# A fused two-block transformer kernel: units and modulation sums of the first attention in other steps, the index weights' product by held weights, the final row sums behind the key's, and the last expert row set mixed singly

## Chip, cores and metric

One NeuronCore of a Trainium2 chip. The metric is device time in microseconds of one execution.

## What is computed

Input is a sequence of 256 tokens with 1024 channels (and 256 context tokens). Two blocks run one after the other. The first: modulated RMS norms, eight-head attention over the tokens and the context with a relative bias, a gated spatial mix beside it, an output projection, two MLPs with squared ReLU and a convolution module between them. The second, cut to what the change touches:

```python
parts = split(modulate(rms_norm(x, norm_attn), sh1, sc1) @ w_in)   # mq mk mv dq dk dv iq ik iw
ik_n = ik * rsqrt(mean(ik * ik) + EPS)
rel = relu(einsum('bqhd,bsd->bqhs', iq, ik_n))
score = einsum('bqh,bqhs->bqs', iw * IDX_HEADS ** -0.5, rel)       # then top-k keys for dsa
...
s = einsum('bthpd,hpnd->bthpn', h @ w_query, sub_keys)             # top 16 of 128 x 128 experts
act = gelu(einsum('btd,bthkd->bthk', h, u_emb[e_idx]))
y = einsum('bthk,bthkd->btd', g * act, v_emb[e_idx])
out = rms_norm(x + g2 * y, norm_final)
```

`mod = silu(c) @ w_ada + b` gives all shifts, scales and gates of the norms.

## The kernel before, in words

Channels lie on the 128 partitions (x is xT, eight tiles of 128 x 256) until the expert stage, where tokens do. Every weight matrix is cut into **units** of 128 x 1024 numbers, two to a transfer of 1 MB into four slots of `ring` (SP's queue). A product is made in three passes of a shortened type: ScalarE converts the unit's high part (L1083, `WB<-ring`), DVE subtracts it from the weights for the low part (L473, the **split**), and TensorE multiplies high by high, high by low and low by high (`rows`, L1570 to L1572: 24 products of 256 columns; `toks_unit`, L1610 to L1612: 12 of 512). WB holds three units, so conversion and split run up to three units ahead (`ahead`), in program order on each engine, and each waits for the product of three units back.

The 128 **modulation sums** of this part (L458, `mods`) are DVE's: a slice of 128 x 1024 weights times a row, added up. `beside[i]` says how many stand behind the split at unit i. Two slices come in one transfer of 1 MB into slots 4 and 5 of `ring`, asked for when the slice pair before last has been used.

The **first attention** runs in 18 steps of `head_steps`, written once for each engine: in step i TensorE makes the scores of head i (L1726), turns the exponentials of head i-1 (L1733) and multiplies those of head i-2 by the values (L1741). DVE adds the bias and takes the maximum (L631, L634), ScalarE copies the context half (L1175) and takes the exponential (L1183); the turned tile is copied by ScalarE (even heads) or DVE (odd ones, L639). Behind a step stands the unit that `fill` names: the gate's (w_in block 1: g, a gelu on ScalarE behind the last), k (block 3), u (block 0), and the first half of the output projection (w_out 0: o0 to o3). `gate_steps` normalises the gate on DVE in steps 5 to 9 (its root is ScalarE's, in step 9), `between_a` mixes it on TensorE in step 11 (L1800), `aside_a` finishes it on DVE (L706, L709), `cat_hi` and `cat_lo` write it as high and low part. `weigh` divides the attention by its sums once a half of the tokens has its last head. The second half of the output projection (o4 to o7) and `into_x` (L693, the residual) follow.

The **index stage** comes behind the norm b2: w_in2 block 6 in units 0 to 3 (iq, iq, ik, iw), ScalarE's eight squares for the last norm "fin", their sum over channels by GpSimd and TensorE (`mean_of_sum`), the key's own row sum (L1898), roots on ScalarE, reciprocals on DVE (L485). iw is made with the tokens' tiles as held weights and four columns (L1907 to L1909: 48 products). Then w_in2 blocks 0, 1 and 2 with `pick_steps` between them, which makes the index scores and finds the chosen keys by eight rounds of maxima.

In the **expert stage** 256 row sets of 1 MB are gathered (L1516), two to a lot. DVE takes the products with the tokens (L1017), ScalarE gelu, gate and a diagonal matrix for both (L1403, L1407, L1413), TensorE adds diagonal times rows up in PSUM (L1973). `finish` makes the residual, the mean square and the scaling of 128 tokens, and SP writes them out.

Numbers of steps, units and heads are counted from 0.

## Time and profile before

| | |
|---|---|
| runs | 1613.29, 1614.20, 1614.34 us; median 1614.2 |
| profiled execution | 1613.14 us; its span 1611.8 us |
| busy, share of the span | PE 88%, DVE 75%, ACT 45%, POOL 21% |
| gathers (software queue) | 268.45 MB, 40.2% of 16 engines |
| other transfers | 207.37 MB, 34.9% |
| mean granted clock of PE | 0.974 |

A row of the timeline has the start, the time busy, the engine, the line of the kernel, the operation with what it writes and reads, how many instructions it merges, and in brackets the idle time before it with what ended it. "PE" is TensorE, "ACT" ScalarE, "POOL" GpSimd, "SPq" an issue of SyncE's queue. Granted clock 1.0 is 2.4 GHz.

### The profile page before, as it was taken

The page shows a single profiled execution, that of the slowest core. Times are in us where ns is not written, and L with a number is a line of the kernel's source. Part 1 is how long each engine was busy: PE and PEld are TensorE (multiplying, and loading weights), DVE is VectorE, ACT ScalarE, POOL GpSimd, SP SyncE. Part 2 cuts the span into 40 slices and gives each one's busy share as a digit, 9 for nine tenths or more (in the row PEclk, how much of TensorE's full clock was granted, in tenths as well). Part 3 has the DMA queues.
Part 4 walks back from the last instruction along what each step waited for, and adds up shares of the span by engine and source line. Part 5 has one row for each costly group of instructions (what it writes and reads, how often), then busy time and mean ns, then how long its engine had stood idle before and what let it go on. Part 6 is the DMA issues. An engine that isn't in the chain of part 4 may idle for free.

```text
span 1611.8 us, 20802 instructions
## 1 busy us (share of the span) xinstructions
PE 1412.7 (88%) x7592; PEld 1034.8 (64%) x7592; DVE 1212.1 (75%) x2373; ACT 728.5 (45%) x1636; POOL 340.1 (21%) x313
## 2 busy tenths in 40 slices
PE   9899899999998999998999879978777777777776
PEld 3777789999987899997878756633332332222222
DVE  6966788887997788877866697877777787777644
ACT  4455365555567655544334544434333333333322
POOL 1100010001000100002001134464444444444430
PEclk9999899999999999998999989999999999999999
DMA  9752359998520499993522369999999999999994
GB/s 390 315 188 79 145 194 337 342 342 313 190 98 3 155 337 339 343 337 108 202 88 103 118 267 419 419 420 420 419 421 420 420 421 420 420 420 419 421 420 208
DMA packets 66055, 477.15 MB, mean 296 GB/s; under 512 B 7329, under 2 KB 7329, under 8 KB 8737
## 3 DMA queue, kind: packets, MB, share of 16 engines
q0 software_dynamic: 36864, 268.45, 40.2%
q1 hardware_dynamic: 29088, 207.37, 34.9%
q8 instruction: 60, 0.98, 0.2%
q14 instruction: 41, 0.34, 0.1%
q10 hardware_dynamic: 2, 0.01, 0.0%
HBM read 474.75 MB, written 1.05 MB: 295 GB/s over the span
## 4 chain that ended last, share of the span: by engine, by line
PE 47%; DMA 27%; DVE 17%; ACT 5%; issue 3%; POOL 1%; ACTq 0%; POOLq 0%; DVEq 0%
DMA row_h<-in_uv,crow 21%; PE ps L1973 7%; PE ps L1570 6%; PE ps L1572 5%; PE ps L1571 5%; DMA row_x<-in_uv,crow 4%; DVE HID L794 4%; PE ps L1854 4%; PE ps L1853 4%; PE ps L1851 4%; DVE WB L473 4%; PE ps L1556 2%; ACT WB L1083 1%; PE ps L1610 1%; DMA ring<-in_stream 1%
## 5 line engine op out<-in xcount | busy, mean ns | idle before, releaser
L473 DVE TENSOR_TENSOR WB<-ring,WB 128x1024 fp32r<-128x1024 f32 x232 | 287.5, 1240 | 92.5 <-ACT WB L1083 89.5
L1083 ACT ACTIVATE WB<-ring 128x1024 fp32r<-128x1024 f32 x232 | 243.4, 1051 | 127.9 <-PE ps L1854 85.1
L1570 PE MATMUL ps<-hH,WB 128*128 128x256 f32 x920 | 268.4, 292 | 7.4 <-DVE WB L473 5.2
L1973 PE MATMUL ps<-ring,P 128*128 128x512 f32 x448 | 214.1, 623 | 66.1 <-ACT P L1413 64.7
L1571 PE MATMUL ps<-hL,WB 128*128 128x256 f32 x920 | 261.5, 284 | 0.0
L1572 PE MATMUL ps<-hH,WB 128*128 128x256 f32 x920 | 261.5, 284 | 0.0
L1973 PEld LDWEIGHTS ps<-ring,P 128*128 128x128 f32 x448 | 84.3, 197 | 189.6 <-ACT P L1413 99.4
L1403 ACT ACTIVATE On<-On 128x2 f32<-128x2 f32 x128 | 26.0, 203 | 377.4 <-DVE On L1017 377.3
L1017 DVE CUSTOM_DVE_ANT_0 ring<-ring,cT 128x1024 f32<-128x1024 f32 x112 | 136.4, 1226 | 76.6 <-DMA ring<-in_uv,crow 75.6
L1570 PEld LDWEIGHTS ps<-hH,WB 128*128 128x128 f32 x920 | 177.6, 193 | 12.7 <-DVE WB L473 6.7
L1571 PEld LDWEIGHTS ps<-hL,WB 128*128 128x128 f32 x920 | 177.8, 193 | 2.2 <-issue 2.2
L1572 PEld LDWEIGHTS ps<-hH,WB 128*128 128x128 f32 x920 | 177.6, 193 | 0.0
L458 DVE CUSTOM_DVE_ANT_0 ring<-ring,crow,cols 128x1024 f32<-128x1024 f32 x128 | 163.3, 1283 | 9.0 <-DMA ring<-in_um 8.8
L1516 POOL DMA_INDIRECT ring<-in_uv,crow x112 | 123.9, 1106 | 202.9 <-PE ps L1973 164.0
L1470 POOL TENSOR_TENSOR sq<-sq 128x256 f32<-128x256 f32 x30 | 33.3, 1110 | 553.6 <-ACT sq L1088 551.6
L1851 PE MATMUL ps<-XB,WB 128*128 128x256 f32 x512 | 144.9, 283 | 0.0
L1853 PE MATMUL ps<-XB,WB 128*128 128x256 f32 x512 | 144.9, 283 | 0.0
L1854 PE MATMUL ps<-XB,WB 128*128 128x256 f32 x512 | 144.9, 283 | 0.0
L1851 PEld LDWEIGHTS ps<-XB,WB 128*128 128x128 f32 x512 | 98.3, 192 | 0.0
L1853 PEld LDWEIGHTS ps<-XB,WB 128*128 128x128 f32 x512 | 98.3, 192 | 0.0
L1854 PEld LDWEIGHTS ps<-XB,WB 128*128 128x128 f32 x512 | 98.3, 192 | 0.0
L1107 ACT ACTIVATE HID<-ps 128x256 f32<-128x256 f32 (+1 forms) x102 | 39.9, 391 | 124.6 <-PE ps L1572 114.3
(297 smaller groups left out, 2775.4 us busy)
## 6 DMA issues: line engine op xcount, KB each, us to landing
ring<-in_stream SPq DMA_DIRECT2D x116, 1024.0 KB, 6.0
ring<-in_um SPq DMA_DIRECT2D x66, 1024.0 KB, 7.3
ring<-in_wm SPq DMA_DIRECT2D x4, 1024.0 KB, 13.0
bias<-in_bias SPq DMA_DIRECT2D x2, 2048.0 KB, 15.2
HID<-in_um SPq DMA_DIRECT2D x4, 512.0 KB, 18.3
ring<-in_uv,crow POOLq DMA_INDIRECT x112, 27.5
xT<-in_xT SPq DMA_DIRECT2D x1, 1024.0 KB, 9.1
cT<-in_cxT SPq DMA_DIRECT2D x1, 1024.0 KB, 14.4
```

Source lines behind the costliest of these rows:

```text
L458: ve.tensor_tensor_reduce(wk, wk, crow[:, layer // 2, :], 1.0, col[f"bm{layer}"][:, m:m + 1], ALU.mult, ALU.add, M[:, layer, m:m + 1]).the ...
L473: ve.tensor_tensor(unit_dst(j, 1), unit_src(j), f(unit_dst(j, 0)), ALU.subtract).then_inc(s_lo, 1)
L1017: ins = ve.tensor_tensor_reduce(u, u, hN[:, n, :], 1.0, 0.0, ALU.mult, ALU.add, dots[:, h, k0 + i:k0 + i + 1])
L1083: se.activation(unit_dst(j, 0), unit_src(j), ACT.Copy).then_inc(s_hi, 1)
L1516: nc.gpsimd.indirect_dma_start(row_ap[row_of[g]], None, A["uv"], bass.IndirectOffsetOnAxis(ap=eu[:, h, k0 + i:k0 + i + 1], axis=0)).then_i ...
L1570: te.matmul(o, wh[:, c], hi[:, kt, :], start=(kt == 0), stop=False)
L1571: te.matmul(o, wh[:, c], lo[:, kt, :], start=False, stop=False)
L1572: mm = te.matmul(o, wl[:, c], hi[:, kt, :], start=False, stop=(kt == 7))
L1851: te.matmul(o, wh[:, c], rH[d % 2][:, k, :], start=(d == 0 and h == 0 and k == 0), stop=False, skip_group_check=True)
L1853: te.matmul(o, wh[:, c], rL[d % 2][:, k, :], start=False, stop=False, skip_group_check=True)
L1854: mm = te.matmul(o, wl[:, c], rH[d % 2][:, k, :], start=False, stop=(d == 7 and k == 3), skip_group_check=True)
L1973: mm = te.matmul(ps[4 + 2 * n + q][:, :], diag[:, g % 8, :], row_ap[row_of[g]][:, 1024 + q * 512:1536 + q * 512], start=(g % 128 == 0), st ...
```

## The change

- First attention: units u2 and u3 stand in steps 10 and 11, not 9 and 10; o0 to o3 in steps 14 to 17 (before 13, 14, 16, 17); the mix's products in step 12, its two halves on DVE in steps 12 and 13 with a tile each; gelu in step 11. The division by the sums stands a step earlier, the low part where it was; in step 17 both parts stand behind the unit. Of the modulation sums, units g0 to g3 have two each (before one), k2, u0, u1 and k3 one each (before none); o1 and o2 have one (before two each on o0 to o4). Units o4 and o5 are split ahead of the residuals.
- Index stage: iw is a `rows` unit with 24 products of 256 columns; its four rows are copied and turned by two small products behind w_in2's first unit. The conversion of the third unit stands ahead of the squares. The key's row sum, root and reciprocal stand ahead of the final norm's. The eight final scalings of x stand two to a unit behind units 1 to 4 of w_in2 blocks 0 and 1, whose eight units have one modulation sum each (before two on the first four); the pick stands ahead of the sum.
- End: of the last lot each row set has its own gelu, gate and diagonal; `finish_last` works in two halves of 512 channels on DVE and ScalarE, and the last 128 tokens go out in two transfers.

```diff
@@ -357,20 +359,20 @@
         beside = [0] * NU
-        for u, n in enumerate((2, 2, 2, 2, 1, 1, 1, 1, 1, 1)):
+        for u, n in enumerate((2, 2, 2, 2, 1, 1, 2, 2, 2, 2, 1, 1, 1, 1)):
             beside[4 + u] = n
-        for u, n in enumerate((2, 2, 2, 2, 2)):
-            beside[first["w_out", 0] + u] = n
+        for u in (1, 2):
+            beside[first["w_out", 0] + u] = 1
         for l in range(2):
             for k in range(48):
                 beside[first[f"ff1_{l}", 0] + 4 + k * 7 // 6] = 1
-        for u in range(4):
-            beside[first["w_in2", 0] + u] = 2
+        for u in range(8):
+            beside[first["w_in2", 0] + u] = 1
         assert sum(beside) == NM
         emptying = []
...
@@ -415,8 +417,8 @@
         fill = {0: [("w_in", 3, 1)], 1: [("w_in", 1, 0)], 2: [("w_in", 1, 1)], 3: [("w_in", 1, 2)], 4: [("w_in", 1, 3)],
-                5: [("w_in", 3, 2)], 6: [("w_in", 0, 0)], 7: [("w_in", 0, 1)], 8: [("w_in", 3, 3)], 9: [("w_in", 0, 2)],
-                10: [("w_in", 0, 3)], 13: [("w_out", 0, 0)], 14: [("w_out", 0, 1)], 16: [("w_out", 0, 2)], 17: [("w_out", 0, 3)]}
+                5: [("w_in", 3, 2)], 6: [("w_in", 0, 0)], 7: [("w_in", 0, 1)], 8: [("w_in", 3, 3)], 10: [("w_in", 0, 2)],
+                11: [("w_in", 0, 3)], 14: [("w_out", 0, 0)], 15: [("w_out", 0, 1)], 16: [("w_out", 0, 2)], 17: [("w_out", 0, 3)]}
...
@@ -638,12 +636,16 @@
                     if due:
-                        out(due.pop())
+                        n = due.pop()
+                        cat_lo(4, n, ps[4 + n][:, :], ("A", n))
                     if i - 2 in last_head:
-                        due.append(last_head.index(i - 2))
+                        n = last_head.index(i - 2)
+                        weigh("A", n, a_pv["A", last_head[n]], a_p["A", last_head[n]])
+                        due.append(n)
+                    aside(i)
                     if i == 17:
-                        out(due.pop())
-                    aside(i)
+                        n = due.pop()
+                        cat_lo(4, n, ps[4 + n][:, :], ("A", n))
                     yield
...
@@ -695,23 +697,24 @@
             def aside_a(i):
-                if i == 11:
+                if i == 12:
                     for n in range(2):
                         p = row_bank(("gmix", n))
                         V.wait_ge(*g_mix[n])
                         V.wait_ge(s_bsp, 16)
-                        V.wait_ge(s_gelu_u, 1)
                         for g in range(4):
                             c = slice(g * 128, g * 128 + 128)
-                            V.then_inc(ve.scalar_tensor_tensor(out=gsq[:, c], in0=p[:, c], scalar=col["lng"][:, g:g + 1],
+                            V.then_inc(ve.scalar_tensor_tensor(out=gsq[n][:, c], in0=p[:, c], scalar=col["lng"][:, g:g + 1],
                                                                in1=bsp[:, c], op0=ALU.mult, op1=ALU.add))
-                        V.wait_own()
+                if i == 13:
+                    V.wait_own()
+                    V.wait_ge(s_gelu_u, 1)
+                    for n in range(2):
                         g_out.then_inc(ve.tensor_tensor(mixed[n].rearrange("p (g c) -> p g c", g=4),
-                                                        gsq.rearrange("p (g c) -> p g c", g=4),
+                                                        gsq[n].rearrange("p (g c) -> p g c", g=4),
                                                         uT[:, :, n * 128:n * 128 + 128], ALU.mult), n)
+                    for n in range(2):
                         V.wait_ge(*g_out[n])
-                if i == 12:
...
@@ -730,7 +733,10 @@
             for u in range(4):
+                if u < 2:
+                    unit(unit_at["w_out", 1, u])
                 into_x(1, u)
+            for u in (2, 3):
...
@@ -860,26 +866,23 @@
-            for u in range(3):
+            for u in range(4):
                 unit(i0 + u)
                 if u == 1:
                     copy_out(("w_in2", 6, 1, 0), iq[:, 1, :], row_bank(("w_in2", 6, 1, 0))[:, 0:256])
-            r1 = rstd("fin")
             r = rstd("ik")
             V.wait_ge(*out_a["w_in2", 6, 2, 0])
             ve.scalar_tensor_tensor(out=ik, in0=ik, scalar=8.0 ** -0.5, in1=r, op0=ALU.mult, op1=ALU.mult).then_inc(s_ik, 1)
-            unit(i0 + 3)
-            for j in range(2):
-                V.wait_ge(*dense["iw", j])
-                out_v.then_inc(ve.tensor_scalar(iw[:, j, :], ps[4 + j][:, 0:4], 0.5, None, ALU.mult), ("iw", j))
-            for kt in range(8):
+            r1 = rstd("fin")
+
+            def fin(kt):
                 x_done.then_inc(ve.scalar_tensor_tensor(out=xT[:, kt, :], in0=xT[:, kt, :], scalar=col["fg"][:, kt:kt + 1],
                                                         in1=r1, op0=ALU.mult, op1=ALU.mult), ("fin", kt))
 
             def pick_steps():
...
@@ -913,8 +916,17 @@
                         copy_out(name, dst[:, u, :], row_bank(name)[:, 0:256])
-                    unit(first["w_in2", b] + u)
+                    i = first["w_in2", b] + u
+                    ahead(i)
+                    if (b, u) == (0, 0):
+                        V.wait_ge(s_iwt, 1)
+                        ve.tensor_scalar(iw, ps[4][:, 0:8].rearrange("p (j c) -> p j c", j=2), 0.5, None,
+                                         ALU.mult).then_inc(s_iw, 1)
                     next(pick, None)
+                    unit(i)
+                    if 1 <= 4 * b + u <= 4:
+                        for kt in range(2):
+                            fin(2 * (4 * b + u - 1) + kt)
...
@@ -1037,6 +1050,26 @@
+
+            def finish_last():
+                ms, halves = sums[:, 63:64], [slice(q * 512, q * 512 + 512) for q in range(2)]
+                for q, c in enumerate(halves):
+                    V.wait_ge(*((s_mix, 256) if q else (s_m0, 1)))
+                    V.then_inc(ve.tensor_tensor(hN[:, 1, c], ps[6 + q][:, :], g2row[:, c], ALU.mult))
+                    V.wait_own()
+                    ve.tensor_tensor(xN[:, 1, c], xN[:, 1, c], hN[:, 1, c], ALU.add).then_inc(s_x1, 1)
+                V.wait_ge(s_nf, 16)
+                for q, c in enumerate(halves):
+                    V.wait_ge(s_x1, q + 1)
+                    V.then_inc(ve.tensor_tensor(hN[:, 1, c], xN[:, 1, c], nfrow[:, c], ALU.mult))
+                    if q == 0:
+                        V.wait_ge(s_sq1, 1)
+                        ve.tensor_scalar(ends_m[0], ends_m[0], EPS, None, ALU.add).then_inc(s_se, 1)
+                V.wait_ge(s_msr, 2)
+                ve.reciprocal(ms, ms).then_inc(s_rms, 1)
+                V.wait_ge(s_rms, 1)
+                V.wait_own()
+                ve.tensor_scalar(xN[:, 1, halves[0]], hN[:, 1, halves[0]], ms, None, ALU.mult).then_inc(s_y, 1)
...
@@ -1336,10 +1369,11 @@
+            i0 = first["w_in2", 6]
+            ahead(i0)
             for kt in range(8):
                 square("fin", kt)
-            i0 = first["w_in2", 6]
-            for u in range(3):
+            for u in range(4):
                 ahead(i0 + u)
...
@@ -1412,6 +1447,32 @@
+            def gelu_last(l):
+                n, h, k0 = LOTS[l]
+                for i in range(2):
+                    k, g = k0 + i, 2 * l + i
+                    S.wait_ge(s_dot, l + i + 1)
+                    S.then_inc(se.activation(dots[:, h, k:k + 1], dots[:, h, k:k + 1], ACT.Gelu))
+                    S.wait_ge(s_gate, 8 * n + h + 1)
+                    S.wait_own()
+                    S.then_inc(se.activation(wts[:, h, k:k + 1], dots[:, h, k:k + 1], ACT.Copy, scale=gates_[:, h, k:k + 1]))
+                    S.wait_own()
+                    S.wait_ge(s_mix, g - 7)
+                    se.activation(diag[:, g % 8, :], ident[:], ACT.Copy, scale=wts[:, h, k:k + 1]).then_inc(s_dg, 1)
+
...
@@ -1890,24 +1950,17 @@
-            for u in range(2, 3):
+            for u in range(2, 4):
                 rows(i0 + u, ("w_in2", 6, u, 0), normed("b2"), (hH, hL))
+            T.wait_ge(s_isq, 1)
+            moment.then_inc(te.matmul(moment_bank["ik"], onesn[:], sq[:, 0, :], start=True, stop=True), "ik")
             mean_of_sum("fin")
-            T.wait_ge(s_isq, 1)
-            T.wait_ge(*r_root["fin"])
-            moment.then_inc(te.matmul(ps[2][:, 0:256], onesn[:], sq[:, 0, :], start=True, stop=True), "ik")
-            i = i0 + 3
-            T.wait_ge(s_lo, i + 1)
-            T.wait_ge(s_hi, i + 1)
-            for j in range(2):
-                r = slice(j * 128, j * 128 + 128)
-                for kt in range(8):
-                    c = slice(kt * 128, kt * 128 + 4)
-                    o = ps[4 + j][:, 0:4]
-                    te.matmul(o, hH[:, kt, r], WB[:, i % 3, 0, c], start=(kt == 0), stop=False)
-                    te.matmul(o, hH[:, kt, r], WB[:, i % 3, 1, c], start=False, stop=False)
-                    mm = te.matmul(o, hL[:, kt, r], WB[:, i % 3, 0, c], start=False, stop=(kt == 7))
-                dense.then_inc(mm, ("iw", j))
+
+            def turn_iw():
+                T.wait_ge(*out_a["w_in2", 6, 3, 0])
+                for j in range(2):
+                    mm = te.transpose(ps[4][:, 4 * j:4 * j + 4], iw_rows[:, 128 * j:128 * j + 128], ident[0:4, 0:4])
+                mm.then_inc(s_iwt, 1)
...
@@ -2088,10 +2145,13 @@
-            for n in range(2):
-                P.wait_ge(s_y, n + 1)
-                sp.dma_start(out[0, n * 128:n * 128 + 128, :], xN[:, n, :]).then_inc(s_out, 16)
-            P.wait_ge(s_out, 32)
+            P.wait_ge(s_y, 1)
+            sp.dma_start(out[0, 0:128, :], xN[:, 0, :]).then_inc(s_out, 16)
+            P.wait_ge(s_y, 2)
+            sp.dma_start(out[0, 128:256, 0:512], xN[:, 1, 0:512]).then_inc(s_out, 16)
+            P.wait_ge(s_y1, 1)
+            sp.dma_start(out[0, 128:256, 512:1024], xN[:, 1, 512:1024]).then_inc(s_out, 16)
+            P.wait_ge(s_out, 48)
```

DVE in step 2 of the first attention, before (L631 and L634 score and maximum, L458 the modulation sum, which the order calls ISA, with its read-out):

```order
L631 SCALAR_TENSOR_TENSOR P<-ps,bias 128x256
L634 TENSOR_REDUCE sums<-P 128x1
L639 COPY PT<-ps 128x512
L473 TENSOR_TENSOR WB<-ring,WB 128x1024
L458 ISA ring,M<-ring,crow,cols 128x1024
L458 ISA M 128x1
L631 SCALAR_TENSOR_TENSOR P<-ps,bias 128x256
```

and in the change:

```order
L629 SCALAR_TENSOR_TENSOR P<-ps,bias 128x256
L632 TENSOR_REDUCE sums<-P 128x1
L637 COPY PT<-ps 128x512
L475 TENSOR_TENSOR WB<-ring,WB 128x1024
L460 ISA ring,M<-ring,crow,cols 128x1024
L460 ISA M 128x1
L460 ISA ring,M<-ring,crow,cols 128x1024
L460 ISA M 128x1
L629 SCALAR_TENSOR_TENSOR P<-ps,bias 128x256
```

A second modulation sum stands between the split and the score of the next head.

DVE around the first unit of the output projection, before (L603 the low part of the mix, L693 the residual):

```order
L603 TENSOR_TENSOR XB<-sq,XB 128x4x128 x2
L631 SCALAR_TENSOR_TENSOR P<-ps,bias 128x256
L634 TENSOR_REDUCE sums<-P 128x1
L473 TENSOR_TENSOR WB<-ring,WB 128x1024
L458 ISA ring,M<-ring,crow,cols 128x1024
L458 ISA M 128x1
L458 ISA ring,M<-ring,crow,cols 128x1024
L458 ISA M 128x1
L693 SCALAR_TENSOR_TENSOR xT<-ps,M,xT 128x256 x2
L631 SCALAR_TENSOR_TENSOR P<-ps,bias 128x256
```

and in the change (L605 the low part, L629 the score, L475 the split, L695 the residual):

```order
L605 TENSOR_TENSOR XB<-sq,XB 128x4x128 x2
L629 SCALAR_TENSOR_TENSOR P<-ps,bias 128x256
L632 TENSOR_REDUCE sums<-P 128x1
L637 COPY PT<-ps 128x512
L475 TENSOR_TENSOR WB<-ring,WB 128x1024
L695 SCALAR_TENSOR_TENSOR xT<-ps,M,xT 128x256 x2
L629 SCALAR_TENSOR_TENSOR P<-ps,bias 128x256
```

The two sums are gone; the score stands behind the low part as before, and a turned head's copy has come in ahead of the split.

DVE in the index stage, before (L870 the key, L874 iw, L876 the final scaling, L890 the pick's first score):

```order
L485 RECIPROCAL rr<-rr 128x256 x2
L870 SCALAR_TENSOR_TENSOR HID<-HID,rr 128x256
L473 TENSOR_TENSOR WB<-ring,WB 128x1024
L874 TENSOR_SCALAR sums<-ps 128x4 x2
L876 SCALAR_TENSOR_TENSOR xT<-xT,cols,rr 128x256 x8
L473 TENSOR_TENSOR WB<-ring,WB 128x1024
L458 ISA ring,M<-ring,crow,cols 128x1024
L458 ISA M 128x1
L458 ISA ring,M<-ring,crow,cols 128x1024
L458 ISA M 128x1
L890 TENSOR_SCALAR cT<-ps,sums 128x128
```

and in the change (L487 reciprocals, L875 the key, L475 the split, L923 iw, L893 the pick, L460 the modulation sum):

```order
L487 RECIPROCAL rr<-rr 128x256
L875 SCALAR_TENSOR_TENSOR HID<-HID,rr 128x256
L487 RECIPROCAL rr<-rr 128x256
L475 TENSOR_TENSOR WB<-ring,WB 128x1024
L923 TENSOR_SCALAR sums<-ps 128x8
L893 TENSOR_SCALAR cT<-ps,sums 128x128
L460 ISA ring,M<-ring,crow,cols 128x1024
L460 ISA M 128x1
L510 COPY HID<-ps 128x256
L475 TENSOR_TENSOR WB<-ring,WB 128x1024
L893 TENSOR_SCALAR cT<-ps,sums 128x128
```

The key's reciprocal is followed by the key at once; the scalings have left this place (they stand two behind a unit from the next one on), and the pick stands ahead of one sum, not behind two.

## Rows read from the trace of the kernel before

**Rows 1.** The page's chain that ended last: shares of the span by line.
```profile
DMA row_h<-in_uv,crow 21%; PE ps L1973 7%; PE ps L1570 6%; PE ps L1572 5%; PE ps L1571 5%; DMA row_x<-in_uv,crow 4%; DVE HID L794 4%; PE ps L1854 4%; PE ps L1853 4%; PE ps L1851 4%; DVE WB L473 4%; PE ps L1556 2%; ACT WB L1083 1%; PE ps L1610 1%; DMA ring<-in_stream 1%
```

**Rows 2.** Windows: stretch, its length, busy us by engine, PEclk, DMA share, GB/s.
```profile
764.25:793.31 29.06, 27.63 (x201) 25.33 (x201) 27.36 (x60) 10.41 (x13) 1.14 (x1) 1.00 0.52 183
1000.00:1100.00 100.00, 88.92 (x319) 49.19 (x318) 79.83 (x201) 45.76 (x133) 49.47 (x43) 0.97 1.01 420
180.00:190.00 10.00, 8.38 (x49) 8.20 (x49) 6.93 (x13) 1.54 (x2) 0.00 (x0) 0.62 0.13 43
190.00:200.00 10.00, 6.92 (x57) 6.53 (x56) 6.68 (x12) 2.62 (x4) 0.00 (x0) 1.00 0.52 200
```

**Rows 3.** Timeline of DVE, first attention: start us, us, engine, line, what, idle before.
```profile
101.25 1.23 DVE L473 TENSOR_TENSOR WB<-ring,WB 128x1024 fp32r<-128x1024 f32 x1 [1.23 <-ACT WB L1083]
...
102.40 1.28 DVE L458 CUSTOM_DVE_ANT_0 ring<-ring,crow,cols 128x1024 f32<-128x1024 f32 x1
...
103.60 0.42 DVE L631 SCALAR_TENSOR_TENSOR P<-ps,bias 128x256 f32<-128x256 f32 x1
...
106.57 1.23 DVE L473 TENSOR_TENSOR WB<-ring,WB 128x1024 fp32r<-128x1024 f32 x1 [1.83 <-ACT WB L1083]
...
146.70 1.23 DVE L596 TENSOR_TENSOR sq<-sq,sums 128x1024 f32<-128x1024 f32 x1
```

**Rows 4.** Timeline of ACT, step 3 of the first attention.
```profile
104.78 0.72 ACT L1183 ACTIVATE P<-P,sums 128x512 f32<-128x512 f32 x1 [1.44 <-DVE sums L634]
```

**Rows 5.** Timeline of PE, first attention: query products, then waits.
```profile
100.99 1.12 PE L1726 MATMUL ps<-HID 64*128 64x512 f32 x2
...
106.29 1.12 PE L1726 MATMUL ps<-HID 64*128 64x512 f32 x2
...
179.07 1.11 PE L1733 MATMUL ps<-ident,P 128*128 128x128 f32 x4 [3.19 <-ACT P L1183]
...
194.53 0.36 PE L1684 MATMUL ps<-XB,WB 128*128 128x256 f32 x1 [1.50 <-DVE XB L603]
```

**Rows 6.** Timeline of ACT, the gate's root in step 9.
```profile
144.83 1.28 ACT L1238 ACT_TABLE_LOAD   x1
146.13 0.30 ACT L1238 ACTIVATE sums<-sums,eps 128x8 f32<-128x8 f32 x1
```

**Rows 7.** Timeline of DVE, last residual of the output projection.
```profile
209.03 0.88 DVE L693 SCALAR_TENSOR_TENSOR xT<-ps,M,xT 128x256 f32<-128x256 f32 x2 [1.31 <-PE ps L1686]
```

**Rows 8.** Timeline of PE: third index unit, w_in2's first unit, its value unit u2.
```profile
746.11 0.39 PE L1570 MATMUL ps<-hH,WB 128*128 128x256 f32 x1 [2.42 <-DVE WB L473]
...
760.83 0.56 PE L1570 MATMUL ps<-hH,WB 128*128 128x256 f32 x1
...
796.57 0.50 PE L1610 MATMUL ps<-WB,hH 128*128 128x512 f32 x1
```

**Rows 9.** The page's DMA issues: a slice of modulation weights, us to landing.
```profile
ring<-in_um SPq DMA_DIRECT2D x66, 1024.0 KB, 7.3
```

**Rows 10.** Timeline of ACT ahead of the third index unit.
```profile
740.82 2.55 ACT L1088 ACTIVATE cT<-xT 128x256 f32<-128x256 f32 x8
```

**Rows 11.** Timeline of DVE, index stage: reciprocals, final scalings.
```profile
751.74 3.54 DVE L485 RECIPROCAL rr<-rr 128x256 f32<-128x256 f32 x2 [2.33 <-ACT rr L1094]
...
761.08 3.25 DVE L876 SCALAR_TENSOR_TENSOR xT<-xT,cols,rr 128x256 f32<-128x256 f32 x8
```

**Rows 12.** Timeline of all engines at the end.
```profile
1594.85 3.70 PE L1973 MATMUL ps<-ring,P 128*128 128x512 f32 x8 [1.25 <-ACT P L1413]
...
1598.62 0.20 ACT L1403 ACTIVATE On<-On 128x2 f32<-128x2 f32 x1 [3.53 <-DVE On L1017]
...
1599.83 3.70 PE L1973 MATMUL ps<-row_h,P 128*128 128x512 f32 x8 [1.27 <-ACT P L1413]
...
1603.56 1.29 DVE L1027 TENSOR_TENSOR cT<-ps,g2row 128x512 f32<-128x512 f32 x2 [4.97 <-PE ps L1973]
...
1609.16 0.34 SPq L2093 DMA_DIRECT2D out<-xN  x1
```

69 lines of the change are left out of this document (42 added, 27 removed).

## The prediction

> **What bounds the kernel now.** I read the chain of waits first, then a table of windows, then each engine's timeline in the three places that the change touches. The chain says that the expert stage is a matter of transfers: 21% of the span goes to rows gathered into row_h alone [rows 1]. In a window inside that stage the transfer engines are busy all the time at 420 GB/s [rows 2]. An expert row set lands every 2.4 us there (1 MB at 420 GB/s, an estimate from that row), however early it was asked for. So what ends the kernel is the time at which the gathers begin, plus a constant, plus what lies behind the last row. Time saved ahead of the gathers should pass through in full; time saved inside that stage is worth nothing; time saved behind its last row counts in full.
>
> Ahead of it TensorE is busy nearly without a gap, except in the first attention's second half and at the index projection. The rows show both.
>
> **First attention, steps 1 to 8: the modulation work that moves in.** In the change, eight of the 24 modulation sums of this stretch leave the output projection: four go in as second sums of steps 1 to 4, four as single ones of steps 5 to 8. DVE's timeline shows the cost of one step: weight split at 101.25, modulation sum at 102.40 (so the split costs 1.15), score at 103.60 (a sum costs 1.20), next split at 106.57 [rows 3]. On ScalarE the exp starts at 104.78 [rows 4]; the conversion of the next weights stands behind it, and the next split behind that. This is a closed loop: split, sum, score, max, exp (1.18 after the score), conversion and next split (1.79 after the exp): 5.32 us. TensorE's own step, 100.99 to 106.29, is 5.30 [rows 5], so the two just match. With two sums the loop is 6.52.
>
> Steps 1 to 4 therefore run ahead of TensorE's need by less and less: the split of step 4 comes at 102.45 + 2 x 6.52 = 115.5 instead of 111.9. The exp of head 3 ends too late for its transpose by 0.7, that of head 4 by a further 1.2, so TensorE enters step 5 1.9 late. Steps 5 to 8 keep one sum each and have the gate's vector operation of 1.23 as well [rows 3]; their loop is 1.15 + 1.20 + 1.2 + 2.97, about 6.55, with a copy in two of them. Walking it on, the exp of head 9 comes near 147.7, and TensorE, which has no projection unit in step 9 now, stands from about 145.4 to 148.65: a wait of 3.2 us that is new. Its unit u2 starts at 150.0 where it started at 141.3, though now with step 10's work.
>
> **Steps 9 to 17: what comes back.** The gelu's table load (1.28 by the root's [rows 6]) moves a step on with unit u3, and the mix's products too. The first out-projection unit then starts near 169.6. Four units follow in four consecutive steps with hardly a stop, since no double sums stand between score and split on DVE and the normalisation by the softmax sums stands a step earlier. Before, TensorE waits 3.19 for the exp of head 14 and 1.50 for the second half's input [rows 5], and for banks behind it; these go, except for about 1.9 ahead of the second half, where the last difference on DVE now stands behind a split and a residual. The second half is then four units of 2.9 with little between them. I get the last residual at 200.2 where the trace has 209.03 [rows 7]: 8.8 us earlier at the full clock.
>
> The clock takes some of it. Right after the 3.19 wait the stretch 180 to 190 has a granted clock of 0.62 [rows 2], so much of it is at 1.2 GHz; after the 2.42 wait at 746 [rows 8] the next units are slower as well. I take one such stretch of some 8 us after the new 3.2 wait. It makes unit u2 3.5 later, of which the ScalarE chain of table loads hides about half: 2.0. A second, short one around the last wait I take at 0.8. **Term 1: -8.8 + 2.8 = -6.0.** Its bounds: -8.8 (no slow stretch) and 0 (the lengthened loop is not made good). The Trainium skill, TensorE: Matmul & The Clock Gate, section on HAM oscillation, says that groups of products divided by waits start at the lower clock time after time; by that the new waits would each cost, and the term would lie nearer its upper bound. The 3.19 row and the 0.62 behind it agree with it; whether the shorter waits count, these rows leave open.
>
> A table load takes 1.28, and the root behind it starts 1.30 after the load did [rows 6]. The Trainium skill, ScalarE: Activation LUTs, section What ACT_TABLE_LOAD costs, gives 2.66 for a switch with its drain; by that the three loads of steps 9 to 12 would put up to 4 us more on the chain and term 1 would be -2. I go by the row.
>
> The transfers of the second sums have room: the slice for step 3 is asked for at 99.5 and needed at 110.1, and the median slice lands 7.3 after its issue [rows 9].
>
> **Index projection.** Before: the third index unit starts at 746.11 after a wait of 2.42 for DVE's split [rows 8], since eight squares of 2.55 us stand ahead of the weights' conversion on ScalarE [rows 10]. Then two row sums, then 48 small products up to 760.83 [rows 8]. In the change one conversion stands ahead of the squares, so this unit starts at 743.6 and ends at 746.5; the fourth, now 24 products with held weights, starts at 747.4 (its bank is released by a DVE copy behind a split) and ends at 750.3; the key's row sum follows at 750.3, the final one at 751.1, and w_in2's first unit at 751.7, some 9 us earlier. The pick's first product no longer waits for anything but the key (ready at 753.7).
>
> DVE takes over as the bound, and this decides the term. It has both reciprocals from 751.74 [rows 11]; in the change it starts the same two at 751.5 and is done with them and the key at 755.4. Before, from the end of the scalings at 764.25 to the split at 793.31, it is busy for 27.4 of 29.06 us [rows 2]; with the gaps of issue between its instructions this is 28.0 us of work. The change keeps this work and puts the eight final scalings of 3.25 [rows 11] in between: 755.4 + 28.0 + 3.25 + 0.2 = 786.8, so 6.5 earlier. TensorE's unit that needs it started at 796.57 [rows 8]; by the same walk it starts at 789.7, so 6.9 earlier, and from there TensorE is the bound again, as before. One modulation sum a unit in place of two changes nothing in the total, since both kinds of unit lie inside this stretch. The waits of about 2 us that TensorE has in it may lower its clock; I take 0.9 for that. **Term 2: -6.0**, bounds -7.3 and -3 (a slow stretch of some 8 us right where TensorE becomes the bound again).
>
> **The tail.** Before, the last two rows' weights come together: gelu at 1598.62, products of both rows 1599.83 to 1603.5 [rows 12]. TensorE is free from 1598.55 (1594.85 + 3.70). In the change the last row but one can be mixed from 1598.55 to 1600.40 and the last from there to 1602.25: 1.28 earlier. Behind it, before, DVE works from 1603.56 until the output goes out at 1609.16 [rows 12]: 5.6 us. In the change halves pipeline: product and addition for half 0 behind the first half of the last product (1601.4 to 1602.7), for half 1 to 1604.0; its square on ScalarE to 1604.9, root 1605.15, reciprocal (behind the norm product) 1605.7, last scaling 1606.3, on two engines. The second output leaves one issue of 0.34 later, at 1606.7: 2.5 earlier than before, and I add 0.1 for its smaller size. **Term 3: -2.6**, bounds -3.3 and -1.3 (only the earlier mix).
>
> **Sum.** -6.0 - 6.0 - 2.6 = -14.6. The profiled execution took 1613.14 (span 1611.8), so 1598.5 for one like it; the median of the runs shown, 1614.2, lies 1.1 higher: 1599.6.
>
> **The rivals.**
> 1. The longer loop of steps 1 to 8 is not made good: term 1 is 0. For it: the loop and TensorE's step match to 0.02, so each of the eight sums is felt somewhere; against it, the out-projection's waits [rows 5] are there to take it up. 1614.2 - 8.6 = 1605.6.
> 2. No slow stretch follows the new waits, and everything walks as at 2.4 GHz: -8.8 - 6.9 - 2.6 = -18.3, so 1595.9.
> 3. Slower: the clock. If the new 3.2 wait in step 9 holds TensorE at 1.2 GHz through to the end of the second half, the work there (eight heads at 2.35, ten units at 2.87, the mix at 2.0: 49.5 at full clock) takes as long again, less the 8 us of waits it fills: +41 against the walk, so 1614.2 - 18.3 + 41 = 1636.9. It decides against the change once the low-clock time exceeds the forecast's by about 29 us. Against it: at 190 to 200 the clock was back [rows 2] although a wait of 1.5 lies there [rows 5]. A milder version gives a result close to no change.
> 4. The index gain is swallowed: the pick's sums on DVE gate the second attention in another order, and only 0 to 1 us of term 2 arrives: 1605. Against it: both feed the same loop and nothing of DVE's is added there.
>
> **How the numbers follow.** Forecast 0.58, rival 1 0.12, rival 2 0.13, rival 3 0.05 (half of it within 0.2%), rival 4 0.07, and 0.05 for a mix of 1 and 4 near 1611, within or just outside 0.2%. The forecast's own spread from the bounds is about 1596 to 1604. The range 1594.8 to 1606.6 takes in rivals 1 and 2 and leaves out about 0.13. A measurement of this kernel can tell 0.2% (3.2 us) from no change. Faster 0.91, same 0.05, slower 0.04.
>
> **What would show it.** In the changed profile: DVE's splits in steps 2 to 4 some 6.5 apart; TensorE's wait for an exp of about 3 us near 145, and whether the clock drops behind it; the last first-attention residual near 202 to 204; w_in2's first unit near 746 (751.7 less what term 1 gives); 420 GB/s from the first full gather window on; first and last row sets of the mix 1.85 apart; the last output issued some 8 us after the last gelu, where it was 10.5. It is wrong if the gathers begin earlier by 12 us and the end does not, or if the first attention ends later than 209.

## The result and the profile after

| | before | changed |
|---|---|---|
| median of the runs | 1613.74 us (1612.52 to 1614.34, 4 runs) | 1597.92 us (1595.59 to 1599.38, 4 runs) |
| ratio | | 0.9896, 95% interval 0.9883 to 0.9908 |
| profiled execution, span | 1613.14, 1611.8 | 1597.58, 1596.3 |
| granted clock of PE, mean | 0.974 | 0.978 |

The changed kernel takes 15.8 us less by the medians (their quotient is 0.9902, inside the interval) and 15.5 by the two spans. The forecast was 14.6 less, 1599.6, with a range of 1594.8 to 1606.6.

Laid side by side, the traces say where the 15.5 went. The output projection's last residual starts 6.0 earlier, though the first query product starts 1.0 later (84.34 and 85.34); over all traces of this study that start lies anywhere from 84.1 to 85.7, so the 1.0 is chance. The stand-in products ahead of the index stage (products whose result nobody reads, which TensorE makes while a norm is being worked out) start 5.9 earlier, the last pick product 12.1, the first row mix 12.1, the last gelu 12.2, the last output issue 15.2. So the three places have 5.9, 6.2 and, with what lies behind the last issue, 3.3.

Windows of the changed kernel, columns as in [rows 2]: two stretches behind new waits, the two that answer to 180 to 200, and the gathers.

```profile
118.50:123.80 5.30, 5.28 (x25) 5.30 (x26) 3.44 (x7) 4.18 (x7) 0.00 (x0) 0.50 0.92 340
151.00:155.00 4.00, 4.00 (x21) 4.00 (x22) 2.35 (x4) 3.09 (x4) 0.00 (x0) 0.57 0.54 223
180.00:190.00 10.00, 9.73 (x84) 9.49 (x82) 9.92 (x17) 2.85 (x5) 0.00 (x0) 1.00 0.49 170
190.00:200.00 10.00, 8.77 (x73) 8.80 (x74) 5.15 (x8) 3.93 (x8) 1.20 (x2) 1.00 0.46 156
1000.00:1100.00 100.00, 88.86 (x297) 47.39 (x296) 74.55 (x177) 42.89 (x127) 52.38 (x46) 0.97 1.01 420
```

The gathers move 420 GB/s as before. The low clock has changed places, and there is less of it. Before, there were two stretches in the first attention, the one that the prediction names and one ahead of it:

```profile
160.50:167.00 6.50, 6.29 (x30) 6.30 (x31) 3.94 (x6) 3.71 (x9) 0.00 (x0) 0.50 0.00 0
177.50:188.50 11.00, 7.81 (x39) 7.42 (x40) 6.49 (x10) 2.36 (x4) 0.00 (x0) 0.54 0.30 115
```

Read in steps of 1 us, TensorE spends 17.1 us of the first attention at the lower level (1.2 GHz) before and 10.2 in the change, there in two stretches near 120 and 153. What stands around them is in the timeline of PE, first attention:

```profile
109.05 0.66 PE L1793 MATMUL ps<-ident,P 128*128 128x128 f32 x4 [0.65 <-ACT P L1216]
...
115.58 0.66 PE L1793 MATMUL ps<-ident,P 128*128 128x128 f32 x4 [1.15 <-ACT P L1216]
...
118.52 0.55 PE L1630 MATMUL ps<-hH,WB 128*128 128x256 f32 x1 [1.45 <-ACT sq L1140]
...
150.99 0.97 PE L1793 MATMUL ps<-ident,P 128*128 128x128 f32 x4 [1.54 <-ACT P L1216]
...
172.38 0.36 PE L1744 MATMUL ps<-XB,WB 128*128 128x256 f32 x1 [0.51 <-DVE XB L605]
...
191.23 0.35 PE L1744 MATMUL ps<-XB,WB 128*128 128x256 f32 x1 [1.50 <-DVE XB L605]
```

Three of these answer to the prediction's walk: 0.65 and 1.15 (forecast 0.7 and 1.2), and the wait of step 9 (1.54, forecast 3.2). The wait of 1.45 does not stand in it. The unit k2 waits there for a bank, which ScalarE empties with the gelu of the gate's last unit, and this gelu stands behind the late exp and a table load. The clock falls at 117.0, between the waits of 1.15 and 1.45, so which of the two brings the stretch is not shown. Of the two waits of [rows 5], the one of 3.19 is gone, and the one of 1.50 stands as before (191.23).

Index stage, timelines of PE and then of DVE in the changed kernel:

```profile
738.86 0.36 PE L1630 MATMUL ps<-hH,WB 128*128 128x256 f32 x1 [1.04 <-ACT HID L1140]
...
746.14 0.47 PE L1630 MATMUL ps<-hH,WB 128*128 128x256 f32 x1
...
771.13 0.38 PE L1630 MATMUL ps<-hH,WB 128*128 128x256 f32 x1 [1.77 <-DVE WB L475]
...
784.50 0.50 PE L1670 MATMUL ps<-WB,hH 128*128 128x512 f32 x1
```

```profile
745.82 1.75 DVE L487 RECIPROCAL rr<-rr 128x256 f32<-128x256 f32 x1 [0.66 <-ACT rr L1127]
747.61 0.42 DVE L875 SCALAR_TENSOR_TENSOR HID<-HID,rr 128x256 f32<-128x256 f32 x1
747.95 1.74 DVE L487 RECIPROCAL rr<-rr 128x256 f32<-128x256 f32 x1
...
756.37 0.88 DVE L879 SCALAR_TENSOR_TENSOR xT<-xT,cols,rr 128x256 f32<-128x256 f32 x2
```

The third index unit (738.86) no longer waits 2.42 for a split, but 1.04 for ScalarE's copy out of a bank, which the walk left out (743.6 less term 1's 6.0 gives 737.6). w_in2's first unit starts at 746.14 (forecast 746; before 760.83 [rows 8]) and the value unit u2 at 784.50 (796.57 before): 12.1 earlier, of which 5.9 were there at the stage's start. Behind the wait of 1.77 the clock falls once:

```profile
772.50:775.50 3.00, 3.00 (x16) 3.00 (x16) 2.93 (x7) 0.00 (x0) 0.00 (x0) 0.50 0.81 322
```

The end of the changed kernel, timelines of PE, ACT, DVE and SP's queue one after the other, beside [rows 12]:

```profile
1586.15 3.60 PE L2028 MATMUL ps<-row_h,P 128*128 128x512 f32 x8
...
1586.40 0.20 ACT L1455 ACTIVATE On<-On 128x1 f32<-128x1 f32 x1 [1.42 <-DVE On L1029]
...
1588.93 0.69 DVE L1058 TENSOR_TENSOR cT<-ps,g2row 128x512 f32<-128x512 f32 x1 [2.56 <-PE ps L2028]
...
1593.05 0.49 DVE L1072 TENSOR_SCALAR xN<-cT,sums 128x512 f32<-128x512 f32 x1
...
1593.56 0.34 SPq L2151 DMA_DIRECT2D out<-xN  x1
1593.95 0.43 SPq L2153 DMA_DIRECT2D out<-xN  x1
```

From the last gelu to the last issue it is 7.55 us, where it was 10.54.

### The profile page after: what moved, and what is told of

It reads as the page before. It is cut to its first block, busy times and chain, and to the rows that moved or that the text cites. A ratio compares the mean times of both kernels' runs of the same rounds, so it can differ in the third digit from the quotient of the medians.

```text
span 1596.3 us, 20768 instructions
## 1 busy us (share of the span) xinstructions
PE 1404.0 (88%) x7570; PEld 1027.3 (64%) x7570; DVE 1209.4 (76%) x2374; ACT 732.0 (46%) x1644; POOL 342.1 (21%) x313
## 3 DMA queue, kind: packets, MB, share of 16 engines
q0 software_dynamic: 36864, 268.45, 40.6%
HBM read 474.75 MB, written 1.05 MB: 298 GB/s over the span
## 4 chain that ended last, share of the span: by engine, by line
PE 45%; DMA 26%; DVE 20%; ACT 5%; issue 3%; POOL 2%; DVEq 0%; POOLq 0%; ACTq 0%
DMA ring<-in_uv,crow 11%; DMA row_x<-in_uv,crow 8%; PE ps L2028 8%; PE ps L1630 5%; PE ps L1631 5%; PE ps L1632 5%; DVE WB L475 4%; DVE HID L800 4%; PE ps L1914 4%; PE ps L1913 4%; PE ps L1911 4%; DMA row_w<-in_uv,crow 4%; DMA row_h<-in_uv,crow 2%; PE ps L1616 2%; ACT WB L1116 2%
## 5 line engine op out<-in xcount | busy, mean ns | idle before, releaser
L475 DVE TENSOR_TENSOR WB<-ring,WB 128x1024 fp32r<-128x1024 f32 x232 | 286.9, 1237 | 95.1 <-ACT WB L1116 92.0
L1630 PE MATMUL ps<-hH,WB 128*128 128x256 f32 x928 | 271.4, 292 | 9.2 <-DVE WB L475 4.5
L1632 PE MATMUL ps<-hH,WB 128*128 128x256 f32 x928 | 264.3, 285 | 0.0
L1630 PEld LDWEIGHTS ps<-hH,WB 128*128 128x128 f32 x928 | 179.7, 194 | 14.9 <-DVE WB L475 7.8
L1632 PEld LDWEIGHTS ps<-hH,WB 128*128 128x128 f32 x928 | 179.9, 194 | 0.0
L460 DVE CUSTOM_DVE_ANT_0 ring<-ring,crow,cols 128x1024 f32<-128x1024 f32 x128 | 163.1, 1279 | 7.6 <-DMA ring<-in_um 7.3
L1140 ACT ACTIVATE HID<-ps 128x256 f32<-128x256 f32 (+2 forms) x103 | 40.2, 391 | 122.8 <-PE ps L1632 112.5
## 6 DMA issues: line engine op xcount, KB each, us to landing
bias<-in_bias SPq DMA_DIRECT2D x2, 2048.0 KB, 15.2
```

The lines of the kernel that those rows point to most:

```text
L460: ve.tensor_tensor_reduce(wk, wk, crow[:, layer // 2, :], 1.0, col[f"bm{layer}"][:, m:m + 1], ALU.mult, ALU.add, M[:, layer, m:m + 1]).the ...
L475: ve.tensor_tensor(unit_dst(j, 1), unit_src(j), f(unit_dst(j, 0)), ALU.subtract).then_inc(s_lo, 1)
L1630: te.matmul(o, wh[:, c], hi[:, kt, :], start=(kt == 0), stop=False)
L1632: mm = te.matmul(o, wl[:, c], hi[:, kt, :], start=False, stop=(kt == 7))
```

## The experiments

Each kernel is the changed one with one edit. "From the first qk" is the time from the first query product of the first attention to the last residual of its projection: 117.7 in the trace of the change, 124.7 before. "Index stage" is from the stand-in products of b2 to the last pick product: 64.3 and 70.5. "Second attention" is from there to the stand-in of ffn. (The expectation of index_undone counts the index stage from a point 2 us later; its difference is the same 6.2.) "Loop theory" is the prediction's reading that split, sums, score, exp and conversion follow one another in a closed loop.

How far one trace can be trusted is seen in the six kernels whose first attention is the change's (the change and five of the runs): from the first qk it takes 117.2 in the trace with 6.8 us at the lower clock, 117.6 to 118.3 in four with 10.2 or 10.3, and 118.9 in the one with 13.7.

**The parts, undone one at a time.**

tail_undone: `finish_last` and `gelu_last` out, `finish(1)`, `gelu(127)` and one output transfer back in.

> The changed kernel with the end as before (the last two rows' gelu and diagonals together, one finish over 1024 channels, one output transfer for the last 128 tokens). If the parts add up and the end is worth what the two traces show (last output issued 7.55 us behind the last gelu against 10.54, and 0.3 less behind the issue), this takes 3.0 to 3.3 us more than the changed kernel, 1601.0 to 1601.2, with the first 1586 us of the trace unchanged. Rival: the end is bound by the transfer of the last rows and the difference between the two traces is chance; then it is 0 to 1 us more, near 1598.5.

1601.27 us (1599.18 to 1602.99), ratio 0.9916 [0.9900, 0.9932]: 3.35 more than the change, about what the traces showed; by the runs alone the two kernels overlap a little (the change's highest is 1599.38). In its trace the issue is 10.54 behind the last gelu again.

finish_undone: the single gelus stay, the halves go.

```diff
-            finish_last()
+            finish(1)
```

> The changed kernel with its single gelus of the last lot, but the finish as before (1024 channels at once on DVE, one output transfer). In the trace of the change the last product ends near 1589.7; the old finish took 5.6 us from there to the issue (1603.56 to 1609.16), so the output would be issued at 1595.4 instead of 1593.95, and it takes 0.3 longer to land: 1.7 us of the tail's 3.3 come from the halves and 1.6 from mixing the last row but one ahead, and this kernel takes 1599.6. Rival: the last dot product sets the end and the mix hides behind it; then the halves bring all of the 3.3 us, 1601.2.

1600.43 us, ratio 0.9909 [0.9890, 0.9928], 2.5 more. The rows of DVE and the issue, in this kernel:

```profile
1591.51 1.29 DVE L1040 TENSOR_TENSOR cT<-ps,g2row 128x512 f32<-128x512 f32 x2 [3.44 <-PE ps L2029]
...
1597.11 0.34 SPq L2150 DMA_DIRECT2D out<-xN  x1
```

Its last gelu is at 1588.11, so DVE's finish starts 3.40 behind it (before 4.94, in the change 2.53) and the issue comes 9.00 behind it (10.54, 7.55). Single gelus bring 1.54 of the issue's 2.99, the halves 1.45 and the shorter landing, about as expected. By the runs alone, 2.5 us is within the spread; the trace carries this reading.

index_undone: the whole index stage, ScalarE's order and w_in2's sums as before.

> The changed kernel with the index stage as before (iw with held tokens, squares ahead of the weights' conversion, the final norm's sum ahead of the key's, the eight scalings in one piece, two sums on each of four units). If the index stage brings its 6.2 us by itself (moment of b2 to last pick product: 68.6 us before, 62.2 in the change), the kernel takes 1604.1, and the stand-in for b2 starts at 726.8 as in the change. Rival: part of the 6.2 is a start of the stage in another phase of the weights' transfers, which the earlier first attention gives; then the cost of undoing it is 3 to 5 us, 1601 to 1603.

1605.71 us (1602.84 to 1608.16), ratio 0.9943 [0.9927, 0.9960], 7.8 more. The stage takes 69.97, 5.7 more than in the change. Another 1.4 us are lost in the second attention (109.8 against 108.4), whose instructions are the same. TensorE is at the lower clock for 10.2 us of it, where it is 6.8 in the change. The stretch that is added stands behind a wait of 1.19:

```profile
853.86 0.66 PE L1767 MATMUL ps<-ident,On 128*128 128x128 f32 x4 [1.19 <-DVE On L614]
```

```profile
855.80:859.30 3.50, 3.50 (x19) 3.50 (x18) 2.77 (x5) 1.64 (x6) 0.00 (x0) 0.53 0.17 66
```

conversion_undone: the conversion of the third unit back behind the squares.

```diff
             i0 = first["w_in2", 6]
-            ahead(i0)
             for kt in range(8):
```

> The changed kernel with the conversion of the third index unit behind the eight squares again. TensorE's wait of 2.42 us ahead of that unit comes back, and with it the start of everything behind it, key included. Theory of the prediction: DVE is the bound from the key on, and its work starts 2.4 us later, so the last pick product is 2.4 later from the stand-in of b2 (66.7 in place of 64.3) and the kernel takes 1600.3. With the clock: before, the stretch of 10 us behind this wait had a granted clock of 0.58 and the change has none such; if the wait of 2.42 brings it back, TensorE's own work there is 3 to 4 longer, and 4 to 6 us are lost in all, 1602 to 1604. Rival: the squares have slack on DVE's side and nothing is lost: 64.3, 1597.9.

1602.42 us (1599.92 to 1604.01), ratio 0.9927 [0.9914, 0.9940], 4.5 more. The wait of 2.42 is back, the stage is 66.6, 2.34 longer, as the walk had it. The second attention takes 112.6 in place of 108.4; against this the index stage began 1.7 earlier than in the change's trace. Two windows behind the wait in this kernel, and the low one of index_undone:

```profile
738.00:748.00 10.00, 9.43 (x63) 9.33 (x64) 6.04 (x6) 4.36 (x8) 4.17 (x3) 0.83 0.38 126
748.00:758.00 10.00, 10.00 (x77) 9.22 (x76) 9.86 (x17) 3.77 (x6) 0.00 (x0) 1.00 0.33 128
```

```profile
751.00:761.00 10.00, 10.00 (x48) 9.67 (x48) 6.78 (x15) 1.81 (x3) 0.00 (x0) 0.55 0.29 105
```

The wait by itself brings a short low stretch here (740.0 to 743.3). The long low one is only in the two kernels that make iw by 48 narrow products, and it begins within them.

pick_behind_sum: the modulation sum ahead of the pick's step again. (The expectation names the split too; it stands ahead of the pick in both kernels.)

```diff
-                    next(pick, None)
                     unit(i)
+                    next(pick, None)
```

> The changed kernel with split and modulation sum ahead of the pick's step again in each of the eight units of w_in2 blocks 0 and 1. Theory of the prediction: DVE has the same work in this stage whatever its order, so nothing changes: 0 to 0.5 us, last pick product 64.3 to 64.8 from the stand-in of b2, 1598. Rival: the pick is the chain that ends the stage, and each of its steps stands 1.2 us later behind the sum: 1 to 3 us, up to 1601.

1598.29 us (1597.13 to 1599.86), ratio 0.9906 [0.9892, 0.9920]; the stage takes 64.3. Nothing changes beyond the noise, as it should be if DVE's total is what counts and not its order: this part of the change is worth nothing that can be measured here.

first_attention_undone: units, mix, division, sums and projection of the first attention as before.

> The changed kernel with the first attention, its sums and its output projection as before. The traces give 5.9 us at the end of the first attention, of which 1.0 is against the change and lies ahead of the first scores already (84.34 before, 85.34 in the change), so undoing it costs 5.9 (1603.8) if that 1.0 comes with the moved sums, and 6.9 (1604.8) if it is chance. The last residual should start at 209.0. Rival: the gain made ahead of the gathers does not pass through in full; then it is under 5 us.

1608.84 us (1607.12 to 1610.17, 8 runs), ratio 0.9964 [0.9953, 0.9976], 10.9 more, outside both theories. The first attention is 124.9 from the first qk, 7.3 more than in the change. Another 3.3 are outside it: the index stage takes 66.2 where it took 64.3 (a granted clock of 0.87 from 783 to 796, behind a wait of 2.14 at 790.5), the second attention 109.9, with 10.2 us at the lower clock.

The three parts undone cost 3.4, 7.8 and 10.9, together 22.0 where the change brings 15.8. They don't add up because low stretches of the clock come and go in stages that a run does not touch. From the last residual to the stand-in of b2, where no kernel here was edited, it is 523.4 to 523.7 in the traces without such a stretch and 525.2 to 526.0 in those with one of 3.4 us.

**How much of the first attention is the sums?**

sums_undone: the order as changed, the modulation sums where they were.

```diff
-(2, 2, 2, 2, 1, 1, 2, 2, 2, 2, 1, 1, 1, 1)
+(2, 2, 2, 2, 1, 1, 1, 1, 1, 1)
...
-        for u in (1, 2):
-            beside[first["w_out", 0] + u] = 1
+        for u, n in enumerate((2, 2, 2, 2, 2)):
+            beside[first["w_out", 0] + u] = n
```

> The changed kernel with the order of the units, the mix and the division by the softmax sums as changed, but the modulation sums of the first attention where they were before (one on each gate unit, none on k2, u0, u1, k3, two on each of o0 to o4). Theory of the prediction: the double sums between score and split are what costs in steps 14 to 17, so they cost there again: four steps of 6.5 in place of 5.3, plus what stands behind, 4 to 5 us, of which the waits of steps 3 to 5 that go (0.65, 1.15 and 1.45 in the trace of the change, and 2.3 of slow products behind them) give a part back only if the projection is not held by something later: I expect the last residual at 205 to 208 and 1600 to 1603. Rival A: the order of the units alone is what gains, and the sums cost wherever they stand: last residual near 203, 1598. Rival B: the moved sums are a loss by themselves: last residual at 198 to 200, 1593 to 1595.

1599.87 us (1598.34 to 1605.13), ratio 0.9912 [0.9895, 0.9930]. From the first qk it is 119.3. So the order of the units alone brings 5.4 of the 7.0, and the moved sums 1.6, by one trace each. TensorE is at the lower clock for 6.8 us here; the trace of the change's first attention with the same 6.8 (conversion_undone) takes 117.2, which makes the sums 2.1. Two of the six runs took 1604.6 and 1605.1, the profiled one among them, and four 1598.3 to 1600.1. This kernel comes to the score of head 15 eight us sooner than the change (82.2 from the first qk against 90.1) and loses more than that in the projection, where DVE's line of splits, double sums and residuals makes TensorE wait. Timeline of PE in sums_undone:

```profile
185.71 0.55 PE L1773 MATMUL ps<-ident,On 128*128 128x128 f32 x3 [1.74 <-DVE On L612]
...
190.73 0.55 PE L1744 MATMUL ps<-XB,WB 128*128 128x256 f32 x1 [4.37 <-DVE XB L605]
```

sums_later: second sums of g0 to g3 on u2 and u3 instead.

```diff
-(2, 2, 2, 2, 1, 1, 2, 2, 2, 2, 1, 1, 1, 1)
+(2, 2, 2, 2, 1, 1, 1, 1, 1, 1, 1, 1, 1, 1, 2, 2)
```

> The changed kernel with the second sums of g0 to g3 moved to u2 and u3, two each, where its DVE is busy for 3.2 of 7 and 3.7 of 6 us. Loop theory: the four double sums stretch the loop of steps 1 to 4 to 6.5 us, and of this come TensorE's waits of 0.65, 1.15 and 1.45 in steps 4 and 5 and the slow products (0.213 instead of 0.119 us apart, 2.3 us over a unit) behind them. Then here the qk of step 5 and that of step 6 lie 8.3 apart as before (13.5 in the change), the unit of step 10 starts 4 to 5 us earlier from the first qk, the two double loops of steps 10 and 11 give 2 to 3 back at head 12's exp, and the last residual starts 115 to 116 from the first qk (117.7 in the change): 1595.5 to 1596.5. Rival: the first attention's end is set by what stands behind step 13 (mix, turn, halves), so nothing of it arrives: 117.7 and 1597.9. Second rival: the sums of steps 10 and 11 cost as much as those of steps 1 to 4, since exp of head 12 is late by 3 us or more: 118 to 120.

1599.36 us, ratio 0.9908 [0.9894, 0.9923], 119.3 from the first qk: the second rival. The query products of heads 5 and 6 lie 8.3 apart, as the loop theory says. But in step 9 the wait is 2.05, and the mix waits for DVE's copy of u3, behind the sums. Timeline and window of sums_later:

```profile
161.47 2.08 PE L1860 MATMUL ps<-wsp,sq 128*128 128x128 f32 x8 [2.51 <-DVE HID L510]
```

```profile
162.00:172.00 10.00, 10.00 (x34) 6.65 (x32) 8.50 (x20) 6.16 (x13) 0.00 (x0) 0.50 0.34 143
```

The low stretch at this new wait lasts from 160.7 to 174.3; with it, what was won is gone. sums_earlier, below, has no such wait and 6.8 us in place of 13.6 at the lower clock, and keeps the gain; how much is the wait and how much the clock was not tried apart.

sums_spread: g0 to g3, u1, k3, o1, o2, o4, o6 one each, u2 and u3 two, k2 and u0 none (the first clause of the expectation names u1 for u0; the list in it is what ran).

> As the run before, but k2 and u1 with none (k3 and u1 keep theirs, u0 none) so that two of them go to the first and third unit of the output projection's second half, behind whose splits DVE waits for TensorE (1.8 and 1.1 us in the trace of the change): one sum each on g0 to g3, u1, k3, o1, o2, o4 and o6, two each on u2 and u3, none on k2 and u0. Loop theory: steps 5 to 9 are relieved by two more sums, so TensorE's wait for the exp of head 9 shrinks by 2.4, and the last residual starts 113 to 115 from the first qk, 1593 to 1595. Rival: the sums on o4 and o6 stand ahead of residuals that release the banks of o5 to o7, so what is won is given back there: 115 to 117.

1603.81 us (1599.02 to 1604.62), ratio 0.9928 [0.9916, 0.9941], 118.1 from the first qk. The wait of step 9 shrinks from 2.05 to 0.34, the wait of 2.51 stays. The first attention is no shorter than in the change, and four of six runs are 4 to 5 us above the other two (see below).

sums_earlier: the second sums on the two units ahead of g0, and two on u2.

```diff
-(2, 2, 2, 2, 1, 1, 2, 2, 2, 2, 1, 1, 1, 1)
+(2, 2, 2, 2, 2, 2, 1, 1, 1, 1, 1, 1, 1, 1, 2)
```

> The changed kernel with one modulation sum on each of g0 to g3, a second one on each of the two units ahead of them (DVE is free there from 77.5 to 84, though the slice pairs land only 1 us ahead of their use) and two on u2, none on u3. Loop theory: the waits of steps 4 and 5 go (as in the run with the sums later), and the 2.5 us wait for DVE's copy of u3 ahead of the mix goes as well, since no sum stands ahead of it: last residual 113 to 115.5 from the first qk, 1593 to 1596. Rival (it holds whatever is done with the sums so far: 117.7, 119.3, 119.3, 118.1): what is won in steps 1 to 9 is waited for later, at the root with its table load or at a slow stretch behind a new wait, and the last residual stays at 117 to 119. Second rival: the added slices are late and the first qk starts 1 to 2 us later.

1597.28 us (1596.25 to 1598.70), ratio 0.9895 [0.9880, 0.9911]; 115.7 from the first qk, and the first qk no later than elsewhere (85.11). The loop theory's upper end: 2.0 us are gained in the trace of the first attention against the change's, and 1.5 against the shortest of the six. The median is within the noise of the change's; in the trace 1.5 of the 2.0 are lost again ahead of the stand-in of b2 (525.2 where the change has 523.7), in a part with the same instructions.

**The clock in the second attention.** Of the twelve traces up to here seven have a second attention of 108.4 to 108.5, two 109.8 or 109.9, three 112.5 or 112.6. The time at the lower clock goes with it: 6.8 us in the seven, 10.2 in the two, 17.1 in the three. TensorE has the same instructions and the same wait of 1.36 us (1.35 before) in all. In the three, the stretch that is added begins in this wait. First the changed kernel, then sums_undone; timeline of PE and the windows behind:

```profile
875.82 0.66 PE L1773 MATMUL ps<-ident,On 128*128 128x128 f32 x4 [1.36 <-DVE On L612]
```

```profile
874.76:878.76 4.00, 2.73 (x22) 2.45 (x23) 3.04 (x7) 3.09 (x7) 0.00 (x0) 1.00 0.00 0
878.76:882.76 4.00, 3.81 (x32) 3.57 (x31) 2.02 (x3) 0.16 (x1) 0.00 (x0) 1.00 0.15 20
```

```profile
879.18 1.12 PE L1773 MATMUL ps<-ident,On 128*128 128x128 f32 x4 [1.36 <-DVE On L612]
```

```profile
878.10:882.10 4.00, 2.92 (x14) 2.80 (x15) 2.69 (x7) 3.11 (x7) 0.00 (x0) 0.59 0.00 0
882.10:886.10 4.00, 4.00 (x21) 4.00 (x21) 1.95 (x4) 0.00 (x0) 0.00 (x0) 0.50 0.00 0
878.90:889.10 10.20, 9.91 (x47) 9.80 (x48) 4.33 (x8) 2.54 (x6) 0.00 (x0) 0.50 0.13 35
```

The same four turns take 0.66 in one and 1.12 in the other. So I filled the wait of sums_spread with three products that nothing reads (spread_filled):

```diff
                         if j == e + 3:
+                            if j == 16:
+                                T.wait_ge(*p_s[14])
+                                for _ in range(3):
+                                    te.matmul(s_pair(j)[:, 0, 0:256], ones[:], bsp[:, 0:256], start=True, stop=True)
                             turn_out(a, n)
```

> As the run with the sums spread, but TensorE's wait of 1.36 us for DVE in the second attention (ahead of the turn of the last attention's first half) is filled with three products of 256 columns into a score bank that is free then (0.44 us each by the six full ones of 5.31; they add nothing to the output). In the traces so far the same wait with the same work behind it left the granted clock at 1.00 in some runs and was followed by 0.50 in others; from the stand-in of b2 to that of ffn the traces took 172.7 in the first case and 176.7 in the second, and of the six runs of the spread kernel four took 1603.2 to 1604.6 and two 1599.0 and 1599.6. Clock theory: with the wait filled all runs are of the shorter kind, 1599 to 1600, with 172.7 to 173.0 in the trace. Rival: the low stretch has its cause further ahead (the wait of 1.8 some 17 us before, or how long the work ahead of it lasted), and both kinds still appear: median 1602 to 1604. Second rival: the three products delay the turn, and 0.3 to 1 us is lost in every run.

1600.10 us (1597.57 to 1600.54), ratio 0.9906 [0.9890, 0.9923]: 3.7 below sums_spread, and none of four runs is of the longer kind. Timeline of PE in spread_filled, and its window:

```profile
877.36 1.51 PE L1818 MATMUL ps<-bsp,ones 128*128 128x256 f32 x6
878.88 0.65 PE L1773 MATMUL ps<-ident,On 128*128 128x128 f32 x4
```

```profile
881.80:885.80 4.00, 3.83 (x33) 3.59 (x31) 2.03 (x3) 0.14 (x1) 0.00 (x0) 1.00 0.13 23
```

The three products stand as six records. The wait is gone, the clock stays at 1.00 (the higher of its two levels, 2.4 GHz), and from the stand-in of b2 to that of ffn it is 172.7, the second attention 108.5. That the wait brings the long stretch is supported, not shown: with 4 of 6 runs long, four short ones could still be chance.

earlier_filled: sums_earlier with the same filling.

> As the run with the sums earlier, with the same wait filled. That kernel's five runs were all of the shorter kind (1596.25 to 1598.7), so the clock theory expects the same time here, 1596.5 to 1597.5, and at most a smaller spread; the rivals expect 0.3 to 1 us more, or a run of the longer kind near 1601. It is also the candidate for a version that beats the changed kernel: two us are gained in its trace by the end of the first attention (115.7 from the first qk in place of 117.7).

1597.09 us (1595.50 to 1597.46), ratio 0.9890 [0.9874, 0.9907]. This is the lowest median of all kernels here, 0.8 below the change, which these intervals cannot tell from it.

## Why the prediction was right

**What bounds the kernel: right.** 12.1 us won ahead of the gathers arrive as 12.2 at the last gelu, and the 3.3 at the end arrive in full. (A row set is 1.05 MB by the 268.45 MB of all 256, so one lands every 2.5 us, an estimate, and not 2.4; nothing hangs on it.)

**Term 1, -6.0: right in size, in part by luck.** The traces give 5.9 with a start that was 1.0 late by chance, 7.0 from the first qk, and 7.3 with the part undone. Its mechanism holds in the first half: splits 6.5 apart (96.93, 103.46, 109.98, 116.50), waits of 0.65 and 1.15 at the steps named. Two steps failed. The walk left out that the late exp delays the gelu, and this the bank of k2: a wait of 1.45, with a low stretch of 6.8 us that begins just ahead of it. TensorE was then itself late, so the new wait of step 9 was 1.54 and not 3.2, with 3.5 us and not eight at the low clock. (With the same code it was 7 us in tail_undone, 149 to 156.) The two errors cancel: the first out-projection unit starts at 172.38 (walk 169.6, plus 2.0 for the clock and 1.0 of start). The second step is the reason given for the return: it was put down to the double sums leaving the projection. The order of the units does most of it, 5.4 of 7.0, the moved sums 1.6, or about 2 at equal clock. The walk also does not name the second low stretch of the kernel before (160.3 to 167.0). From 17.1 to 10.2 us at half the clock is work worth up to 3.4 us, as an estimate, so a part of the 7.0 is the clock. That the longer loop is "made good" is right, but it costs what it was priced at, and a placement that spares it wins 1.5 to 2.0 more in the trace.

**The table loads: the row held.** Timeline of ACT in the changed kernel, ahead of the last square:

```profile
1587.38 1.28 ACT L1131 ACT_TABLE_LOAD   x1
1588.68 0.20 ACT L1131 ACTIVATE eps<-eps 128x1 f32<-128x1 f32 x1
```

The figure of 2.66 for a switch that the Trainium skill gives (ScalarE: Activation LUTs, What ACT_TABLE_LOAD costs) would have made term 1 -2; by these rows the activation starts 1.30 after the load did, with nothing between them, and the load of the gate's root in step 9 is the same (150.96, root at 152.25). The Trainium skill's page adds its figure up from 1.283 for the load, with which the trace agrees, and a drain of 1.38, which it does not show.

**Term 2, -6.0: right.** 6.2 in the traces. DVE's two reciprocals (forecast 745.5 with term 1, measured 745.82) and w_in2's first unit are where the walk had them. TensorE's third unit is 1.3 late for the copy that the walk left out; the fourth unit follows it without the gap that the walk allowed, so the key's row sum is only 0.4 late (744.69). The value unit comes at 784.50, where the walk had 783.7 with term 1: 6.2 and not 6.9. Of the 0.7, 0.4 is a slip of the sum, which has the split ahead of this unit 6.5 earlier and the unit itself 6.9, and no row for the difference; the rest is about the lateness of the key's row sum. conversion_undone loses the 2.34 that it gave that step, and in pick_behind_sum the order on DVE is worth nothing. The 0.9 taken for the clock has nothing to stand for: the clock did fall once, for 3.4 us behind the wait of 1.77, but sums_earlier has no low stretch in this stage and takes the same 64.3. So the term came near by two errors of opposite sign: 0.7 too much in the walk, 0.9 taken off for the clock. The low stretch within the narrow products (0.55 in the row of index_undone) is gone with them. One condition of it was not seen: undone alone, it costs 7.8, of which 5.7 are in the stage and 1.4 in the second attention, which can lose 1.4 to 4.1 to the clock.

**Term 3, -2.6: a little small.** 3.3, the bound. Mixing ahead measured 1.5 for 1.28 and the halves 1.45 for about 1.2 in the issue, and the smaller last transfer lands 0.3 sooner, where the sum allowed 0.1.

**The rivals.** Rival 3, that a new wait holds the clock low for tens of microseconds, did not come: the two low stretches of the first attention are 6.8 and 3.5 us long in the change. Rivals 1 and 4, that term 1 or term 2 comes to nothing, fall with the 5.9 and the 6.2. Rival 2, no slow stretch, is nearly as close in its sum (1595.9, 2.0 too low; the forecast is 1.7 too high) and wrong in its mechanism, since two slow stretches did come. The section on HAM oscillation of the Trainium skill (TensorE: Matmul & The Clock Gate) says that groups of products divided by waits start at the lower clock time after time; its case is waits for transfers, these are waits for other engines. At the 1.45, 1.54, 1.77 and 2.51 waits the traces agree, behind the 0.65 and the second half's 1.50 they do not (1.00 from 190 to 200), and behind the 1.36 wait they agree in some kernels and not in others.

## What to carry to other kernels

Walk the delayed engine's whole queue: a loop that grows by one operation delays not only the next of its kind but the copy that frees a bank somewhere behind. Undo a part and read the stages it did not touch as well: here 3.3 of 10.9 us lay in stages that were the same in both, and the parts undone add up to 22.0 where the whole is 15.8. Next to each time from a trace, write down how long TensorE was at the lower clock in it. A short wait of TensorE that is worth 1.4 us was followed by 4 more in some traces; with dummy products into a free bank in its place none of four runs was long, where four of six had been, at no price seen here.

## What was unexpected of the hardware

The same 1.36 us wait, with the same work ahead and behind, is followed by a granted clock of 1.00 in nine of twelve traces and by 0.50 for about 10 us in three, worth 4.1 us. Two kernels have runs of both lengths (sums_spread 4 long of 6, sums_undone 2 of 6), so whether edits hundreds of microseconds ahead change how often it comes is not shown. What decides it stays open; the runs show only that with the wait of sums_spread filled no long run came (0 of 4, against 4 of 6), and these are few. The 3.3 us beyond the first attention in first_attention_undone are low stretches too, but of some 3.5 us behind other waits (2.14 in the index stage, 1.18 in the second attention); none of those was filled.

A unit of 48 products of four columns, though TensorE was busy throughout, ran into a low stretch of some 10 us in both kernels that have it; the same numbers made with 24 products of 256 columns did not. conversion_undone, with the wait of 2.42 but the wide products, has only the short stretch, which speaks for the narrow products; the small waits just ahead of them (0.66) were not tried apart.
